# A two-block transformer kernel: wide products in five stages, a convolution tap on ScalarE, x parts made earlier

## What is computed

```python
x = x + merged @ w_out                                   # stage wout, 16 panels
h = rms_norm(x, ffn_norm)
up = causal_dwconv(h @ w_up, conv_w, conv_b)             # stage up, 88 panels; 3 taps and a bias
a, b = up[..., :5632], up[..., 5632:]
x = x + (silu(a) * b) @ w_down                           # stage down, not touched
...
z = rms_norm_2(h, mix_norm_gain) @ w_in_2                # stage in2, 17 panels
...
q = rms_norm_2(h, ffn_norm_gain) @ w_pq                  # stage pq, 16 panels
...
gate = sigmoid(rms_norm_2(h, ple_norm_gain) @ w_ple_gate)  # stage pg, 16 panels, the last of the kernel
```

## Time and profile before

| | |
|---|---|
| median of the three runs | 3814.34 us |
| lowest, highest | 3807.51, 3821.97 us |
| the profiled execution | 3821.03 us |
| its span, first to last instruction | 3819.4 us |
| mean granted TensorE clock, share of 2.4 GHz | 0.981 |
| TensorE busy | 3662.8 us, 96% of the span |
| VectorE, ScalarE, GpSimd busy | 2030.6, 1728.6, 1819.9 us |

### The profile page before, as it was taken

How to read it: one execution, slowest core, us unless ns; L and a number is a source line. 1 busy time by engine, 2 the same in 40 slices (tenths; PEclk the granted TensorE clock), 3 DMA queues, 4 the chain that set the end, 5 groups by cost and what they waited for, 6 DMA issues and landing times. The chain is left out here.

```text
span 3819.4 us, 71471 instructions
## 1 busy us (share of the span) xinstructions
PE 3662.8 (96%) x22756; PEld 3290.1 (86%) x22756; DVE 2030.6 (53%) x3303; ACT 1728.6 (45%) x2954; POOL 1819.9 (48%) x1294
## 2 busy tenths in 40 slices
PE   7999999999999999997999999999999999999999
PEld 6888878999899999886958999888888788888889
DVE  5644454445577777335534458655555433333345
ACT  2121154544444444555434455454555455555554
POOL 1001154545455544444315456878777455555533
PEclk9999999999999999998999999999999999999999
DMA  4443343565577665663524555577777777777754
GB/s 156 144 144 120 122 140 126 163 204 164 163 228 226 225 204 169 192 193 119 161 91 132 182 161 175 154 187 185 185 187 185 221 214 220 215 219 215 215 176 160
DMA packets 388737, 672.31 MB, mean 176 GB/s; under 512 B 75968, under 2 KB 76096, under 8 KB 386064
## 3 DMA queue, kind: packets, MB, share of 16 engines
q1 hardware_dynamic: 344304, 630.48, 53.3%
q0 software_dynamic: 44320, 40.32, 5.0%
HBM read 649.53 MB, written 21.10 MB: 176 GB/s over the span
## 5 line engine op out<-in xcount | busy, mean ns | idle before, releaser
L442 ACT ACTIVATE whi<-ring 128x512 fp32r<-128x512 f32 x2108 | 1310.9, 631 | 1311.2 <-PE ps L631 725.0
L455 POOL TENSOR_TENSOR wlo<-ring,whi 128x512 fp32r<-128x512 f32 x724 | 972.2, 1344 | 1096.8 <-ACT whi L442 1096.2
L455 DVE TENSOR_TENSOR wlo<-ring,whi 128x512 fp32r<-128x512 f32 x722 | 583.9, 815 | 917.2 <-ACT whi L442 907.7
L629 PE MATMUL ps<-xhl,whi 128*128 128x256 f32 x3440 | 993.9, 289 | 66.9 <-POOL wlo L455 18.1
L630 PE MATMUL ps<-xhl,whi 128*128 128x256 f32 x3440 | 985.1, 286 | 0.0
L631 PE MATMUL ps<-xhl,wlo 128*128 128x256 f32 x3440 | 984.9, 286 | 0.0
L629 PEld LDWEIGHTS ps<-xhl,whi 128*128 128x128 f32 x3440 | 672.6, 196 | 77.6 <-issue 23.1
L630 PEld LDWEIGHTS ps<-xhl,whi 128*128 128x128 f32 x3440 | 672.7, 196 | 0.2
L631 PEld LDWEIGHTS ps<-xhl,wlo 128*128 128x128 f32 x3440 | 672.2, 195 | 0.0
L733 PE MATMUL ps<-whi,xhl 128*128 128x512 f32 x1376 | 537.5, 391 | 9.4 <-DVE xhl L1223 5.3
L734 PE MATMUL ps<-wlo,xhl 128*128 128x512 f32 x1376 | 537.0, 390 | 0.0
(11 more groups left out here) (231 smaller groups left out, 3987.6 us busy)
## 6 DMA issues: line engine op xcount, KB each, us to landing
ring<-stream SPq DMA_DIRECT2D x2380, 256.0 KB, 3.6
gates<-arena POOLq DMA_DIRECT2D x16, 1024.0 KB, 6.8
arena<-gates POOLq DMA_DIRECT2D x32, 512.0 KB, 6.2
gates<-arena POOLq DMA_INDIRECT x256
res<-xT SPq DMA_DIRECT2D x4, 512.0 KB, 7.2
res<-xT POOLq DMA_DIRECT2D x1, 2048.0 KB, 11.1
outT<-res POOLq DMA_DIRECT2D x1, 2048.0 KB, 7.6
parked<-outT POOLq DMA_DIRECT2D x1, 2048.0 KB, 10.8
```

The lines of the kernel that those rows point to most:

```text
L442: act.activation(quarters(whi, g), quarters(ring[:, n % SLOTS, :], g), ACT.Copy).then_inc(w_hi, 1)
L455: eng.tensor_tensor(quarters(wlo, g), quarters(ring[:, n % SLOTS, :], g), quarters(whi, g).bitcast(F32), ALU.subtract).then_inc(done, 1)
L629: pe.matmul(out, whi[:, b], hi, start=start, stop=False, **kw)
```

## The change

- wout, up, in2, pq and pg use the wide form (153 panels); `project_wide` learns the waits that `project_split` had.
- The halves of a bank are added: in wout by a second addition into `res`; in in2, pq and pg by a VectorE reduce over 512 columns (`both_halves`) ahead of the multiplication, which then reads SBUF; in up ScalarE copies the second half out of PSUM into `fhalf`, VectorE adds the first half to it, then multiplies by `rstd`.
- In up the tensor_scalar for the unshifted tap and the bias leaves VectorE; ScalarE does it with an Identity activation (`last_tap`). VectorE waits for it before the shifted taps. ScalarE's order per panel becomes: quarter 0 of the next panel, the tap of the panel before, quarters 1 and 2, the Silu after odd panels, quarter 3, the copy of the second half.
- Merged x parts: ScalarE makes each `x_high` after the second tile of a turn, not the fourth; GpSimd makes x rests 0 and 2 within its merge panels, VectorE x rest 1 after tile 12. Only x rest 3 stays at the end.
- Four mLSTM semaphores become two, with the same waits. Counters of the loops follow.

The diff, with most unchanged lines left out, indentation reduced, and the hunks for semaphores and loop counters left out:

```diff
@@ -334,7 +334,7 @@
 gff = area2(0, FT * T)
-fa, fb, fx = (area2((FT + k) * T, T) for k in range(3))
+fa, fb, fx, fhalf = (area2((FT + k) * T, T) for k in range(4))
 rows1 = area2(0, 2 * D)
...
@@ -648,31 +648,38 @@
             middle()
-def project_wide(n, p, i):
-    pe.wait_ge(evac_done, turn(i, 4, p - 3))
+def project_wide(n, p, i=None, name=None, x=xhl, tiles=None, middle=None):
+    if i is not None or p >= 4:
+        pe.wait_ge(evac_done, turn(i, 4, p - 3))
     for g in range(4):
         quarter_ready(n, g, i, 4)
+        if name:
+            pe.wait_ge((x_lo_pool, x_lo_dve)[g % 2], XQ[name] // 2 + g // 2 + 1)
         for k in range(4 * g, 4 * g + 4):
             b, t = slice(k * P, (k + 1) * P), slice(k * T, (k + 1) * T)
-            pe.matmul(ps[:, p % 4, :], whi[:, b], xhl[:, :, t], start=(k == 0), stop=False, skip_group_check=True)
-            mm = pe.matmul(ps[:, p % 4, 0:T], wlo[:, b], xhi[:, t], start=False, stop=(k == KD - 1),
+            if tiles:
+                pe.wait_ge(t_lo, TILES[tiles] + k + 1)
+            pe.matmul(ps[:, p % 4, :], whi[:, b], x[:, :, t], start=(k == 0), stop=False, skip_group_check=True)
+            mm = pe.matmul(ps[:, p % 4, 0:T], wlo[:, b], x[:, 0, t], start=False, stop=(k == KD - 1),
                            skip_group_check=True)
         mm.then_inc(quarter_used if g < 3 else panel_done, 1)
-def split_loop(n, p, count, name=None, tiles=None, middle=None):
+        if middle and g == 1:
+            middle()
+def split_loop(n, p, count, name=None, tiles=None, middle=None, form=project_split):
     done = 1 if name or tiles else 0
     if done:
-        project_split(n, p, name, tiles=tiles, middle=middle)
+        form(n, p, name=name, tiles=tiles, middle=middle)
     turns = (count - done) // 4
...
             for j in range(done, done + 4):
-                project_split(n + j, p + j, None, i)
+                form(n + j, p + j, None, i) if form is project_split else form(n + j, p + j, i)
     for j in range(done + 4 * turns, count):
-        project_split(n + j, p + j, None)
+        form(n + j, p + j, name=None)
 def project_loop(n, p, count, src, first=None):
...
@@ -709,15 +716,6 @@
     mm.then_inc(rms_ss, 1)
-def split_residual(n, p, name, r, sq):
-    x = parts_of(name)
-    for j in range(4):
-        project_split(n + j, p + j, name if j == 0 else None, x=x)
-    with pe.Fori(0, 3) as i:
-        for j in range(4, 8):
-            project_split(n + j, p + j, None, i, x=x)
 def accumulate_all(n, count, tiles_before):
...
@@ -965,27 +963,32 @@
         merge(m, i)
-split_residual(PANELS["wout"], OUT["wout"], "merged", 1, nx())
-project_split(PANELS["up"], OUT["up"], None, tiles="ffn")
-project_split(PANELS["up"] + 1, OUT["up"] + 1, None, middle=lambda: folded_sums(1, nx()))
-split_loop(PANELS["up"] + 2, OUT["up"] + 2, 2 * FT - 2)
+merged_parts = mhl[:].rearrange("p (a t) -> p a t", a=2)
+for j in range(4):
+    project_wide(PANELS["wout"] + j, OUT["wout"] + j, name=None if j else "merged", x=merged_parts)
+with pe.Fori(0, 3) as i:
+    for j in range(4, 8):
+        project_wide(PANELS["wout"] + j, OUT["wout"] + j, i, x=merged_parts)
+project_wide(PANELS["up"], OUT["up"], tiles="ffn")
+project_wide(PANELS["up"] + 1, OUT["up"] + 1, middle=lambda: folded_sums(1, nx()))
+split_loop(PANELS["up"] + 2, OUT["up"] + 2, 2 * FT - 2, form=project_wide)
 pe.wait_ge(S["ff_out"], FT)
...
 pe.wait_ge(S["res_done"], OUT["in2"] % 4 + 1)
-project_split(PANELS["in2"], OUT["in2"], None, tiles="mix2")
-project_split(PANELS["in2"] + 1, OUT["in2"] + 1, None)
+project_wide(PANELS["in2"], OUT["in2"], tiles="mix2")
+project_wide(PANELS["in2"] + 1, OUT["in2"] + 1)
 folded_sums(2, sq_final)
 folded_sums(3, nx(), 5)
-split_loop(PANELS["in2"] + 2, OUT["in2"] + 2, 9)
+split_loop(PANELS["in2"] + 2, OUT["in2"] + 2, 9, form=project_wide)
 sum_squares(4, sq, 4)
-split_loop(PANELS["in2"] + 11, OUT["in2"] + 11, 3)
+split_loop(PANELS["in2"] + 11, OUT["in2"] + 11, 3, form=project_wide)
 sum_squares(5, sq[:, 4 * T:8 * T], 4, 5)
-split_loop(PANELS["in2"] + 14, OUT["in2"] + 14, 3)
+split_loop(PANELS["in2"] + 14, OUT["in2"] + 14, 3, form=project_wide)
 o = 0
...
@@ -1158,9 +1161,9 @@
         half_panel(j, g)
-project_split(PANELS["pq"], OUT["pq"], None, tiles="ffn2")
-project_split(PANELS["pq"] + 1, OUT["pq"] + 1, None, middle=lambda: folded_sums(6, sq_attn))
-split_loop(PANELS["pq"] + 2, OUT["pq"] + 2, KD - 2)
+project_wide(PANELS["pq"], OUT["pq"], tiles="ffn2")
+project_wide(PANELS["pq"] + 1, OUT["pq"] + 1, middle=lambda: folded_sums(6, sq_attn))
+split_loop(PANELS["pq"] + 2, OUT["pq"] + 2, KD - 2, form=project_wide)
 n = PANELS["subk"]
...
@@ -1200,10 +1203,10 @@
     pe.wait_ge(S["pp_ev"], 4)
-    project_split(PANELS["pg"], OUT["pg"], None, tiles="ple")
+    project_wide(PANELS["pg"], OUT["pg"], tiles="ple")
     pe.wait_ge(S["pp_ev"], 5)
-    project_split(PANELS["pg"] + 1, OUT["pg"] + 1, None, middle=lambda: folded_sums(7, nx()))
-    split_loop(PANELS["pg"] + 2, OUT["pg"] + 2, KD - 2)
+    project_wide(PANELS["pg"] + 1, OUT["pg"] + 1, middle=lambda: folded_sums(7, nx()))
+    split_loop(PANELS["pg"] + 2, OUT["pg"] + 2, KD - 2, form=project_wide)
 @block.vector
...
@@ -1227,6 +1230,10 @@
     return dve.scalar_tensor_tensor(out, a, s, b, op0, op1)
+def both_halves(out, p):
+    return dve.tensor_reduce(out, ps[:, p % 4, :].rearrange("p (a t) -> p t a", a=2), AX.X, ALU.add)
 rms_c = {k: Count(dve, s) for k, s in (("ms", rms_ms), ("out", rms_out))}
...
@@ -1279,7 +1288,8 @@
     c = res[:, j * T:(j + 1) * T] if i is None else res[:, bass.ds(i * (4 * T) + j * T, T)]
-    evac.link(tt(c, c, ps[:, p % 4, 0:T], ALU.add))
+    L(tt(c, c, ps[:, p % 4, 0:T], ALU.add))
+    evac.link(tt(c, c, ps[:, p % 4, T:2 * T], ALU.add))
 def panel_of(p):
...
@@ -1541,8 +1551,9 @@
     gather(m)
+    if m == 12:
+        x_rest(dve, "merged", merged, 1)
 merge(KD - 1)
-x_rest(dve, "merged", merged, 1)
 rests(dve, PANELS["wout"])
...
@@ -1564,9 +1575,11 @@
 w = (lambda c: par[:, at + c:at + c + 1] if i is None else par[:, bass.ds(i * 16 + (at + c), 1)])
-dve.wait_ge(panel_done, turn(i, 4, PANELS["up"] + 2 * u + half + 1))
-evac.link(tt(fx, ps[:, p % 4, 0:T], rstd[:], ALU.mult))
-L(ts(f, fx, w(2), w(3), ALU.mult, ALU.add))
+copied = 2 * (2 * u + half) + 1
+dve.wait_ge(S["ff_act"], turn(i, 8, copied))
+L(tt(fx, ps[:, p % 4, 0:T], fhalf, ALU.add))
+evac.link(tt(fx, fx, rstd[:], ALU.mult))
+dve.wait_ge(S["ff_act"], turn(i, 8, copied + 1))
 L(stt(f[:, 1:T], fx[:, 0:T - 1], w(1), f[:, 1:T], ALU.mult, ALU.add))
...
@@ -1654,7 +1667,8 @@
 dve.wait_ge(panel_done, PANELS["in2"] + j + 1)
-evac.link(tt(z2t(IN2[j]), ps[:, (OUT["in2"] + j) % 4, 0:T], r12, ALU.mult))
+L(both_halves(z2t(IN2[j]), OUT["in2"] + j))
+evac.link(tt(z2t(IN2[j]), z2t(IN2[j]), r12, ALU.mult))
 if j < KD:
...
@@ -1770,7 +1784,9 @@
     dve.wait_ge(panel_done, PANELS["pq"] + j + 1)
-    evac.link(tt(q2[:, j * T:(j + 1) * T], ps[:, (OUT["pq"] + j) % 4, 0:T], rstd[:], ALU.mult))
+    q = q2[:, j * T:(j + 1) * T]
+    L(both_halves(q, OUT["pq"] + j))
+    evac.link(tt(q, q, rstd[:], ALU.mult))
 def normal(k):
...
@@ -1919,7 +1935,8 @@
         dve.wait_ge(S["gate_act"], turn(i, 4, j - 1))
-    evac.link(tt(gx[j % 2], ps[:, j % 4, 0:T], rstd[:], ALU.mult))
+    L(both_halves(gx[j % 2], j))
+    evac.link(tt(gx[j % 2], gx[j % 2], rstd[:], ALU.mult))
 def finish(j, i=None):
...
@@ -2183,33 +2200,65 @@
         gate(m, i)
-    act.wait_ge(S["merged_done"], i * 4 + 4)
-    x_high(act, "merged", 0, merged, i)
+        if m == 5:
+            act.wait_ge(S["merged_done"], i * 4 + 4)
+            x_high(act, "merged", 0, merged, i)
     evac.leave(3)
...
 high_and_squares(PANELS["wout"] + 1, OUT["wout"], "ffn", nx())
-N["ff_silu"] = Count(act, S["ff_silu"])
-def ffn_pair(u, i=None):
-    high_parts(act, PANELS["up"] + 2 * u + 1, i, 4)
-    high_parts(act, PANELS["up"] + 2 * u + 2, i, 4)
-    if u == 0:
-        root(1)
+N["ff_silu"], N["ff_act"] = Count(act, S["ff_silu"]), Count(act, S["ff_act"])
+def second_half(k, i=None):
+    act.wait_ge(panel_done, turn(i, 4, PANELS["up"] + k + 1))
+    tell("ff_act", fn(fhalf, ps[:, (OUT["up"] + k) % 4, T:2 * T], ACT.Copy))
+def last_tap(k, i=None):
+    act.wait_ge(evac_done, turn(i, 4, OUT["up"] + k + 1))
+    at = COL["fconv"] + 4 * k
+    w = (lambda c: par[:, at + c:at + c + 1] if i is None else par[:, bass.ds(i * 16 + (at + c), 1)])
+    tell("ff_act", fn((fa, fb)[k % 2], fx, ACT.Identity, scale=w(2), bias=w(3)))
+def silu(u, i=None):
     act.wait_ge(S["ff_conv"], turn(i, 2, u + 1))
     tell("ff_silu", fn(fa, fa, ACT.Silu))
-for u in range(2):
-    ffn_pair(u)
+def up_panel(k, i=None):
+    n = PANELS["up"] + k + 1
+    high_quarter(act, n, 0, i, 4)
+    last_tap(k - 1, i)
+    if k == 2:
+        silu(0)
+    for g in (1, 2):
+        high_quarter(act, n, g, i, 4)
+    if k % 2:
+        silu(k // 2, i)
+    high_quarter(act, n, 3, i, 4)
+    second_half(k, i)
+high_parts(act, PANELS["up"] + 1)
+second_half(0)
```

(43 more changed lines are left out.)

12 lines of the change are left out of this document (6 added, 6 removed).

## The result

The changed kernel takes **3879.28 us** (median of 4 runs, 3877.44 to 3881.17); the kernel before 3813.01 us (4 runs). The ratio is **1.0172**, 95% interval 1.0159 to 1.0185: 66 us slower. The forecast was 3795 us, so it was wrong in sign; of its rivals the one called wholly bound (3832 us, chance 0.08) comes nearest, and it is 47 us short of the result. The profiled execution of after has a span of 3879.4 us, against 3819.4.

The account below looks back on a forecast made before the run. TensorE, busy in 96% of the span, was taken as the bound. Terms -15.8 + 1.3 - 4.7 - 5.4 + 0.5 - 1.8 + 0.4 + 6.7 = -18.8 us took 3821.0 profiled to 3802.2; median forecast 3795, range 3780 to 3813.

Parts of the forecast that it names:

- wholly bound: Up: new product held while GpSimd works, VectorE's round 6.1 us against 5.65 a panel; 3832 us, chance 0.08.
- the term: Steady up, 84 panels: the wide products' gain of 9.0 us, within a forecast -15.8.
- so 4.1 of 5.65: Up: VectorE's work per panel after the change, 4.1 us, against TensorE's 5.65 us of products.
- It fits, with 0.3 us left in odd panels: Up: VectorE's next remainder ends at 5.4 us, or 6.8 where GpSimd interferes; TensorE needs it at 7.07.
- the right ring: Up: round from VectorE to ScalarE and back once a panel, summed to 6.1 us against 5.65.
- place: Up: slowdown located in VectorE to ScalarE and back once a panel, ScalarE's next copy queued behind the tap.
- the milder rival: Up: VectorE's remainder 0.3 us late in every odd panel, +12.6 in place of +1.3; 3807 us, chance 0.19.
- Into wout: Merge's end to wout's first panel: earlier x quarters shorten TensorE's wait, -5.4 us, bounds 0 and -7.1.
- Inside wout: Wout's loop: wait per turn grows from 0.4 to 1.0 us, eating 12 panels' saving, 0; second up panel's chain +0.5.
- Start of up: Before up's first Silu: ScalarE converts a quarter earlier, TensorE's wait at 1014.90 ends 1.8 us sooner, -1.8 (0 to -3).
- End of up: After up's last panel: the tap's way to ScalarE and back lies open, +0.4 us (0 to +1).
- in2, pq, pg: Extra bank emptying hidden in loops, exposed at stage heads and ends and the kernel's last bank: +6.7 us, bounds +3 and +10.

## Why the prediction was wrong, point by point

**The products were sized right.** With the holds taken away, the steady stretch took 474.85 us where I had 474.9, and wide against narrow, both without holds, is 474.85 against 484.05: 9.2 us, where the term says 9.0. The short waits of the narrow form were 6.5 (I had 6.9). The fixed 2.5 ns of the Trainium skill (TensorE: Matmul & The Clock Gate, Back-to-back issue gap), which the page gives for the isolated gap between two products, would have made 3.4 us of those 9.2, an estimate by that page; the runs stay with the rows.

**The step that failed** is "so 4.1 of 5.65", under "Can the other engines keep up?". VectorE had 5.09 us of work a panel and 0.94 of idle time for the tap, with gaps 6.51 us. Three of its sizes were wrong, and for one reason. The product with rstd was priced at the 0.425 of the pair product, a group of which none in the trace of before begins inside a remainder of GpSimd: 0.98. The pair product itself was kept at 0.425: 1.51. And taking the tensor_scalar off VectorE was booked as 1.08 saved, though its own work is 0.44 (in the kernel before with GpSimd cut) and the other 0.64 was a hold, which stayed and fell on others. The row that showed it was there, and I used it only for the rival. The remainders, booked at 0.93 each, took 1.10. So "It fits, with 0.3 us left in odd panels" was a sum of durations taken at one arrangement in time and used at another.

**The rival "wholly bound"** had the right mechanism, a new tensor_tensor that is held, and nearly the right ring: its sum holds VectorE's whole queue, with both remainders and the tap's 0.50 in it. By the groups above, it had three terms too small: the pair product 0.21 a panel for 0.77, the remainders 1.86 for 2.2, and the tap 0.50 where VectorE idles 0.94; the product with rstd (1.08 for 0.98) and the shifted taps (1.17 for 0.97) were too large. So it gave 6.1 us for 6.51. Its "place", the way to ScalarE and back, was not the cause: the run with GpSimd cut has the same idle time and no loss, and the tap back on VectorE shows that the ring binds without ScalarE, and harder. Its chance of 0.08 was too low. The "against" beside the milder rival, that VectorE loses its most stretched instruction, was the error itself. The Trainium skill (GPSIMD Engine Reference, Specifications) names VectorE instructions with two SBUF inputs; the runs agree for these: 425 ns free and 1.38 held at 1199.77, and 0.42 at 1204.41 as soon as one input is in PSUM. The Trainium skill (SBUF — State Buffer, SBUF: two separate sides) also says that the one who comes second is blocked for the whole instruction of the first; the timeline above agrees, with 1.38 us begun 0.19 behind a remainder of 1.28. Had I applied that rule in the sum, each of GpSimd's two remainders a panel could have cost VectorE up to 1.3 us, an estimate from the 1.28 of that remainder.

**Into wout: right to 0.1 us.** From the merge's last product to wout's second panel 13.02 us became 7.64, -5.4 as forecast, and the wait sits where I put it, before the second quarter:

```profile
883.06 0.49 PE L664 MATMUL ps<-mhl,whi 128*128 128x512 f32 x1 [1.67 <-DVE wlo L455]
```

**Inside wout** +1.5 where the sum had -0.4 (0 for the waits, 0.4 for four panels). The wait at each turn grew as argued but to more, and eats more than the panels save; it answers to the 0.23 at 942.48:

```profile
910.96 0.50 PE L664 MATMUL ps<-mhl,whi 128*128 128x512 f32 x1 [1.28 <-POOL wlo L455]
```

**Start of up**: the wait at its second panel grew by 1.0 (I had 0.5); the wait of 4.49 didn't end 1.8 sooner but split into two of together 4.67:

```profile
1007.06 0.50 PE L664 MATMUL ps<-xhl,whi 128*128 128x512 f32 x1 [2.99 <-POOL wlo L455]
...
1011.16 0.80 PE L664 MATMUL ps<-xhl,whi 128*128 128x512 f32 x1 [1.68 <-DVE wlo L455]
```

**End of up**: +1.2, for +0.4.

**in2, pq, pg**: +9 with the panels' own gain in it, where +6.7 - 4.1 = +2.6 was forecast. The heads of in2 and pg came as said, 5.60 to 7.05 (I had 1.5 more) and 3.25 to 4.08 (0.7 more); so did pq's end, 2.62 to 4.24 (1.45 more). The wait for pq's remainder of quarter 1 is new, 3.19, twice my 1.45. (pq's first product stands at 2123.95 in the trace of before; the 2133 given ahead for its start is that of its second panel.) The lines, in this order:

```profile
1865.58 0.80 PE L664 MATMUL ps<-xhl,whi 128*128 128x512 f32 x1 [7.05 <-DVE wlo L455]
...
2207.28 0.50 PE L664 MATMUL ps<-xhl,whi 128*128 128x512 f32 x1 [3.19 <-DVE wlo L455]
...
2282.50 0.77 PE L1176 MATMUL ps<-ring,arena 128*128 128x128 f32 x2 [4.24 <-DVE arena L1226]
...
3793.73 0.80 PE L664 MATMUL ps<-xhl,whi 128*128 128x512 f32 x1 [4.08 <-POOL wlo L455]
```

And the loops' gain was not had in in2 and pg. From the fifth panel on, in2 took 72.63 us against 72.56, and pg's last eleven panels 65.30 against 63.36, with a short wait at the head of most panels. What took the gain back in in2 stays open. In pg these waits end with GpSimd's remainders, not VectorE's. The two engines make theirs side by side there, and both groups are long (3767 to 3880 us): VectorE's remainder 1366 ns, against 705 where nothing holds it, and GpSimd's 1512, against 1299 in the kernel before (3740 to 3814 us). That this lateness makes the waits is read from these rows, and no run took it away.

```profile
L664 PEld LDWEIGHTS ps<-xhl,whi 128*128 128x128 f32 x256 | 50.1, 196 | 23.9 <-POOL wlo L455 7.9 <-issue 4.2
L455 POOL TENSOR_TENSOR wlo<-ring,whi 128x512 fp32r<-128x512 f32 x31 | 46.4, 1512 | 55.7 <-ACT whi L442 55.7
L455 DVE TENSOR_TENSOR wlo<-ring,whi 128x512 fp32r<-128x512 f32 x32 | 43.4, 1366 | 19.6 <-ACT whi L442 19.1
```

By the text's own test, a panel of 5.8 us or more in up, the forecast fails at the first thing that it named.

## What to carry to other kernels

Where VectorE and GpSimd work side by side, the duration in the profile of a VectorE instruction that reads SBUF alone can be its own time plus a hold, and the hold belongs to the moment, not to the instruction: taking a stretched instruction away hands its hold to the next one. Price VectorE by the durations it has where GpSimd is still, add the overlap with GpSimd as a term of its own, and check the sum against the whole round of its queue, not against one chain. And when a sum of two halves is needed, leave it in PSUM: here the instruction that read it from there was not held.
